# Fifteen low parts of each layer's input projection: subtracted by VectorE behind the evictions instead of by GpSimd

## The reference

```
x = x + concat(A, B, C, D)(rmsnorm(x) @ w_in) @ w_out      # the input projection feeds all four head groups
x = x + square(relu(rmsnorm(x) @ mlp_w1)) @ mlp_w2         # d_ff = 4096
x = x + (p @ ple_w_proj) * sigmoid(rmsnorm(x) @ ple_w_gate)
```

## Time and profile before

| | before |
|---|---|
| median of 3 timed runs | 1674.24 us (1672.52 to 1679.57) |
| the profiled execution | 1675.74 us |
| its span in the profile | 1674.0 us |
| PE busy | 1576.1 us (94%) |
| PE weight loads busy | 1491.3 us (89%) |
| VectorE busy | 909.3 us (54%) |
| ACT busy | 488.9 us (29%) |
| GpSimd busy | 639.6 us (38%) |
| mean granted clock of TensorE | 0.981 |

### The profile page before, as it was taken

One profiled execution on the slowest core, in us unless ns is written; L12 is line 12 of the kernel. 1 busy time (PEld: TensorE's weight loads), 2 busy tenths in 40 slices (PEclk: granted clock), 3 DMA queues, 4 the chain that ended last, 5 costly groups with the idle time before them and its releaser, 6 DMA issues. The chain is left out here.

```text
span 1674.0 us, 32923 instructions
## 1 busy us (share of the span) xinstructions
PE 1576.1 (94%) x14582; PEld 1491.3 (89%) x14582; DVE 909.3 (54%) x1370; ACT 488.9 (29%) x800; POOL 639.6 (38%) x313
## 2 busy tenths in 40 slices
PE   6899999799999999999888999988999999999995
PEld 5789787599999999999887897867999999999995
DVE  6765467546545271654576645764472634527553
ACT  6522233432111111133444313334311111111332
POOL 3235111054444443455532531111633444444652
PEclk9899999899999999999998999998999999999998
DMA  5111010132222232232321110102332222222221
GB/s 191 63 39 40 27 52 26 44 90 85 87 84 88 87 89 89 89 89 78 93 77 51 40 40 28 49 26 58 89 89 88 89 88 89 88 84 87 88 85 66
DMA packets 43804, 122.61 MB, mean 73 GB/s; under 512 B 10960, under 2 KB 13776, under 8 KB 43536
## 3 DMA queue, kind: packets, MB, share of 16 engines
q1 hardware_dynamic: 43520, 118.74, 23.4%
q10 hardware_dynamic: 144, 1.78, 0.3%
HBM read 116.75 MB, written 3.76 MB: 72 GB/s over the span
## 5 line engine op out<-in xcount | busy, mean ns | idle before, releaser
L1329 PE MATMUL psum_p<-hidden,w_high 128*128 128x272 f32 x5952 | 1003.6, 290 | 17.8 <-POOL w_rest L567 7.9
L1329 PEld LDWEIGHTS psum_p<-hidden,w_high 128*128 128x128 f32 x5952 | 847.3, 189 | 24.0 <-POOL w_rest L567 11.7
L567 POOL TENSOR_TENSOR w_rest<-raw,w_high 128x1024 fp32r<-128x1024 f32 x210 | 512.5, 2441 | 903.2 <-ACT w_high L650 903.2
L1329 PE MATMUL psum_p<-hidden,w_rest 128*128 128x272 f32 x2976 | 616.4, 288 | 0.0
L1329 PEld LDWEIGHTS psum_p<-hidden,w_rest 128*128 128x128 f32 x2976 | 466.6, 189 | 0.0
L650 ACT ACTIVATE w_high<-raw 128x1024 fp32r<-128x1024 f32 x210 | 222.6, 1060 | 827.6 <-PE psum_p L1329 791.6
L1166 DVE TENSOR_TENSOR x<-psum_p,x 128x544 f32<-128x544 f32 x80 | 58.0, 725 | 280.9 <-PE psum_p L1329 280.9
L918 DVE CAST hidden<-rope 128x544 fp32r<-128x544 f32 x64 | 157.3, 2458 | 2.2
L913 DVE SCALAR_TENSOR_TENSOR hidden<-x,parameters,hidden 128x544 fp32r<-128x544 f32 x48 | 92.9, 1935 | 45.3 <-ACT hidden L667 45.1
L1179 DVE SCALAR_TENSOR_TENSOR rope_in<-psum_p,rms 128x544 f32<-128x544 f32 x64 | 46.4, 725 | 109.2 <-PE psum_p L1329 100.6
L579 POOL TENSOR_TENSOR x_squares_summed<-x_squares_summed,x_squared 128x544 f32<-128x544 f32 x43 | 72.5, 1687 | 53.9 <-ACT x_squared L673 47.2
(11 more groups left out here) (249 smaller groups left out, 1392.3 us busy)
## 6 DMA issues: line engine op xcount, KB each, us to landing
raw<-w_units SPq DMA_DIRECT2D x210, 512.0 KB, 3.5
x<-x_t SPq DMA_DIRECT2D x8, 272.0 KB, 6.2
y_t<-y SPq DMA_DIRECT2D x8, 272.0 KB, 2.1
constants<-consts ACTq DMA_DIRECT2D x1, 1737.5 KB, 7.6
ple_in<-p_t SPq DMA_DIRECT2D x2, 544.0 KB, 4.8
w_kv<-w_kv SPq DMA_DIRECT2D x2, 256.0 KB, 5.2
ckv_p<-mla_c SPq DMA_DIRECT2D x2, 256.0 KB, 2.7
mla_c<-ckv_cache SPq DMA_DIRECT2D x2, 128.0 KB, 5.1
```

What stands on the lines that cost most here:

```text
L567: mark(pool.tensor_tensor(wlo[:, s, :], raw[:, ring(l, u, RAW), :], whi[:, s, :].bitcast(F32), ALU.subtract), lo_done)
L1329: ins = pe.matmul(pp[:, 2 * b + h, 0:HALF], w[:, s, cols(k)], rhs[:, k, part, h * HALF:(h + 1) * HALF], start=(n == 0 and z == 0), stop=(n ...
```

## The change

The low parts of units 2 to 16 of each layer are no longer computed by GpSimd. A function of the same name for VectorE waits for the high part of unit u+2 and subtracts; `evacuate` calls it behind the last piece of the eviction of unit u for u below 15, and `in_tile` calls it for the two latent query units, which have an eviction of their own. The semaphore is the same. GpSimd keeps its hooks, waits once until these fifteen are done, and goes on with unit 17. Units 0 and 1, and all from 17 on, stay with GpSimd.

```diff
@@ gpsimd
                 for u in range(N_PRE):
                     mid_unit(l, 2 * u)
-                    rest(l, u + SPLIT)
                     mid_unit(l, 2 * u + 1)
+
+                pool.wait_ge(*lo_done.at(l, N_PRE + SPLIT))
+                lo_done.made += N_PRE
                 for u in range(N_PRE, N_IN):
                     rest(l, u + SPLIT)
@@ vector, evacuate
                     if j == len(pieces) - 1:
                         link(dve, ins, freed, l)
+                if u < N_PRE:
+                    rest(l, u + SPLIT)
@@ vector
+            def rest(l, u):
+
+                dve.wait_ge(*hi_done.at(l, u + 1))
+                s = ring(l, u, SPLIT)
+                dve.tensor_tensor(wlo[:, s, :], raw[:, ring(l, u, RAW), :], f(whi[:, s, :]), ALU.subtract
+                                  ).then_inc(lo_done.sem, 1)
```

## The result

The changed kernel takes 1695.76 us (median of 4 runs, 1694.24 to 1697.24), the one before 1674.57 us in the same comparison (4 runs, 1672.52 to 1679.57): ratio 1.0122, interval 1.0098 to 1.0146. It is slower by 21 us; the interval allows 16 to 24. The forecast was 1694.0, in a range of 1682 to 1706.

The account below looks back on a forecast made before the run. VectorE, not the 94% busy PE, was taken to set the input-projection stage. Terms of +9.1 us (layer 0) and +10.5 (layer 1) sum to +19.6 us, forecasting 1694 us, range 1682 to 1706.

Parts of the forecast that it names:

- VectorE sets this stage, and its waits for ACT replace the old wait: Input projection, up to the l2 sums: VectorE newly waits for ACT's high parts; +5.4 us in layer 0, +6.8 in layer 1.
- the ring: Input projection: convolution, Silu, high part, low part and next convolution wait in turn; ACT's leg 1.85 or 2.85 us.
- p(2) and p(3): Products of units 2 and 3: p(2) waits 1.3 us more, absorbed by p(3)'s wait; rest(3) ends 0.15 us later.
- Price of one: One 1024-wide subtraction on VectorE takes 1.25 us, with ends of 1.2 and 2.44 us.
- rival D: Slower yet: one low-part subtraction takes 2.44 us on VectorE; 1711 us, chance 9%.
- The gate columns: Unit 6: VectorE's shorter unit shrinks PE's wait for the gate columns, -0.5 us a layer.
- Unit 10: GpSimd's level factors start earlier and meet VectorE's latent scaling, ahead of the k_decayed PE needs: +1.0 us a layer.
- The levels: Units 11 to 13: the low part delays level results PE waits for; +1.25, +0.8, +1.2, together +3.2 us a layer.
- Units 7 to 9: Behind these evictions VectorE idles about 2.1 us each, so the 1.25 us subtraction fits at no cost.
- Rival A: Faster: relief of the port shared by VectorE and GpSimd wins, convolution 5 ending before 63.9; 1662.6 us, chance 5%.
- Rival C: High parts come early, so ACT closes no ring and VectorE alone sets the pace: +9.8 us, 1684 us, chance 8%.
- Rival B: No change: high parts come early and PE's third level batches do not wait for later level results; 1678 us, chance 8%.

Follow-up runs that it names:

- the kernel with the convolution first: Changed kernel, but for units 1 to 6 VectorE subtracts the low part behind the convolution instead of ahead of it: 1678.66 us.
- the one with the late squares: Changed kernel, but ACT squares q and k behind the next high part instead of in front of it: 1691.37 us.
- The kernel with two subtractions: Changed kernel, with every subtraction on VectorE made twice in a row: 1730.32 us.
- the run with the waiting factors: Changed kernel, but GpSimd starts the first level's three factors only after VectorE's low part of unit 12: 1694.73 us.
- the kernel with only the six behind the convolution: Kernel before the change, with only low parts 3 to 8 moved to VectorE, behind the convolutions of units 1 to 6: 1668.27 us.
- both orders: Changed kernel, but VectorE subtracts behind the convolution for units 1 to 6 and behind the level results for units 11 to 13: 1674.56 us.

## Why the prediction held, point by point

- **VectorE sets this stage, and its waits for ACT replace the old wait** (+5.4 and +6.8 us forecast): +4.9 and +6.35 measured. By its own steps: rest(3) was to end at 37.8, which with the later start of that run is 39.0; it ended at 38.88. From there to the end of convolution 5, 31.5 us forecast, 31.14 measured (70.02). The ACT legs (1.85 and 2.85 us forecast) took 1.74 and 2.82. That it is the order and not the load is shown by the kernel with the convolution first (the same work, -17 us), and that ACT closes the ring by the one with the late squares (-4.4 us for 2 x 2.17). The prediction gave the sum of the steps but not its split: in layer 1, 4.2 us of the 6.35 come from the first wait, at unit 1, and 2.1 from the rounds behind it. The kernel with two subtractions gives 1.26 us of stretch for each of six rests, rest(2) and rest(3) included.
- **p(2) and p(3).** I said that rest(2) costs 1.3 us on the way to high(3) and rest(3) gives 1.15 back. The run with unit 2 back on GpSimd gives 1.1 us for the first, so the two cancel, as forecast within 0.15 us. The word "absorbed" holds for the sum, not for rest(2): it was worth 2.2 us in two layers.
- **Price of one:** 1.25 us forecast, 1.225 measured, 30 times. The nearest row was the right one to take, and rival D (2.44 us) fell with it. It would have come true with GpSimd working beside: 2.59 us.
- **The gate columns** (-0.5 us a layer): -1.0 and -0.4 measured. The wait itself fell by 0.6 us in both layers (2.44 to 1.85). The rest of it lies in PE's pace behind the third sum: in layer 0 the granted clock of the first 7 us there was 0.71 before and 0.78 after.
- **Unit 10** (+1.0): +0.9 and +0.8, by the mechanism named, as the run with the waiting factors shows (0.75 + 0.25 us instead of 1.03 + 1.00). It returned 0.85 us in each layer.
- **The levels** (+1.25, +0.8, +1.2): the stretches grew by 1.14, 0.75 and 1.18 us. They are independent of the ring, and cured by order alone.
- **Units 7 to 9** at nothing: right for one rest, since the waits there stayed at 0.25 to 0.5 us; two no longer fit. The raw loads, also put at nothing, cost nothing: in the profile after, no high part of this stage waited for a load.
- **PE's restart** was left as it was, and the first four sums take 2.15 us in both kernels although the wait is 10.1 us instead of 5.3.

The sum of 19.6 us was 2 us above the trace's 17.6; half of that excess lies in the first stretch. Against the medians, 21 us, it was 1.6 us too low. That the forecast of 1694 came within 2 us of 1695.76 is therefore partly luck: no term of the sum covers the 3 to 4 us that the profiles do not find. Rival A (the port relief wins) needed convolution 5 before 63.9; it came at 70.02. But its mechanism is real: 2 us for each convolution, as the profile of after shows. It was worth 3.7 us in layer 0 and 2.3 in layer 1, net of the subtractions, in the kernel with only the six behind the convolution. Rival C (highs come early) is refuted by the 24.9 us of waiting for w_high. Rival B fell with the six level waits.

What I had not asked in the prediction is which part of the change is good. Six of the fifteen subtractions, behind the convolution, are worth 6.8 us, some 3 of which may be the clock seen above; the other nine, and the place ahead of the convolution, cost.

## What to carry to other kernels

An instruction that waits for another engine must not stand ahead of the one that this engine is waiting for: before moving work, write down for both engines what is queued behind each wait, and look for a closed ring. Here the larger part, 4.2 us a layer, came from one such wait ahead of a convolution that used to fill the time, and 1.2 us from each round in which the other engine had extra work in its leg, although the moved operation became twice as fast and its new engine was half idle. When a move helps by one mechanism (a stretched operation becomes short) and hurts by another (order), try it behind the work that others wait for before giving it up.

## What the hardware showed beyond what was expected

- The exclusion between VectorE and GpSimd covers work with one tensor input too: a tensor_scalar of 128x547 took 2.63 us instead of 0.49 while GpSimd subtracted. Small instructions are held as well: a scaling of 32 columns took 1.00 us instead of 0.25 beside factors of about 1 us each.
- Doubling the waits before level corrections from 1.0 to 1.2 us to 2.2 to 2.5 us brought the granted clock of the following 6 to 8 us from 1.00 to between 0.72 and 0.79, and made these stretches 1.4 to 1.5 us longer. Behind the wait that grew to 1.79 us the clock stayed at 1.00. Length alone does not fix the cost: behind the same wait of 3.07 us for the squares PE's next four sums took 2.15 us with the six alone, and 1.72 and 1.16 in the two layers with both orders. Which property of the wait decides was not measured.
